# A decoder layer on one core: turning h for the down products by VectorE and a trip through DRAM instead of by TensorE

## The reference

```python
def swiglu(h, w_gate, w_up, w_down):
    return (jax.nn.silu(h @ w_gate) * (h @ w_up)) @ w_down
x = x + 0.5 * swiglu(rmsnorm(x, norm_ffn1[i]), w1_gate[i], w1_up[i], w1_down[i])
```

## Time and profile before

| what | value |
|---|---|
| median of 3 runs | 2013.55 us (2013.05 to 2016.1) |
| the profiled execution's own time | 2014.49 us |
| its span in the profile | 2012.7 us |
| granted TensorE clock, mean | 0.997 |
| PE busy | 1979.8 us (98%) |
| DVE busy | 1506.6 us (75%) |
| ACT busy | 1071.8 us (53%) |
| POOL busy | 233.3 us (12%) |

### The profile page before, as it was taken

One profiled execution on the slowest core, in us unless ns is written; L12 is line 12 of the kernel. 1 busy time (PEld: TensorE's weight loads), 2 busy tenths in 40 slices (PEclk: granted clock), 3 DMA queues, 4 the chain that ended last, 5 costly groups with the idle time before them and its releaser, 6 DMA issues.

```text
span 2012.7 us, 28994 instructions
## 1 busy us (share of the span) xinstructions
PE 1979.8 (98%) x11176; PEld 1638.6 (81%) x11176; DVE 1506.6 (75%) x1324; ACT 1071.8 (53%) x1043; POOL 233.3 (12%) x190
## 2 busy tenths in 40 slices
PE   8999999999999999999898999999999999999999
PEld 6788888888888889888787888888888888888887
DVE  5987787778878755766788546988878777787664
ACT  4655555555555556855344346555555555555553
POOL 0000000000000000344432000000000000000000
PEclk9999999999999999999998999999999999999999
DMA  7587668776787756667312555678766877677854
GB/s 249 195 242 232 215 220 249 230 232 211 235 239 233 216 174 219 198 191 222 120 42 71 173 188 168 197 241 241 237 213 209 250 234 234 211 234 231 239 178 147
DMA packets 214636, 415.69 MB, mean 207 GB/s; under 512 B 11207, under 2 KB 21059, under 8 KB 214557
## 3 DMA queue, kind: packets, MB, share of 16 engines
q1 hardware_dynamic: 189116, 361.48, 52.9%
q0 software_dynamic: 25440, 53.09, 13.9%
HBM read 363.94 MB, written 5.52 MB: 184 GB/s over the span
## 4 chain that ended last, share of the span: by engine, by line
PE 90%; DVE 7%; issue 2%; ACT 1%; DMA 0%; SPq 0%; DVEq 0%; ACTq 0%
PE PS L466 14%; PE PS L468 14%; PE PS L467 14%; PE PS L541 8%; PE PS L543 8%; PE PS L542 8%; PE PS L559 6%; PE PS L558 6%; PE PS L560 6%; PE PS L1638 2%; DVE wlo L426 2%; PE PS L521 1%; PE PS L487 1%; ACT t_hi L448 1%; DVE t_lo L453 0%
## 5 line engine op out<-in xcount | busy, mean ns | idle before, releaser
L426 DVE TENSOR_TENSOR wlo<-raw,whi 128x2048 fp32r<-128x2048 f32 (+2 forms) x338 | 732.5, 2167 | 337.3 <-PE PS L468 271.3
L417 ACT ACTIVATE whi<-raw 128x2048 fp32r<-128x2048 f32 (+2 forms) x338 | 606.0, 1794 | 217.2 <-PE PS L468 137.2
L541 PE MATMUL PS<-whi,xT_hi 128*128 128x512 f32 x768 | 303.8, 396 | 4.9 <-issue 3.2
L543 PE MATMUL PS<-whi,xT_lo 128*128 128x512 f32 x768 | 300.8, 392 | 0.0
L542 PE MATMUL PS<-wlo,xT_hi 128*128 128x512 f32 x768 | 299.4, 390 | 0.0
L466 PE MATMUL PS<-whi,hT_hi 128*128 128x512 f32 x680 | 267.6, 394 | 0.6 <-DVE wlo L426 0.4
L448 ACT ACTIVATE t_hi<-T 128x2048 fp32r<-128x2048 f32 x80 | 153.7, 1922 | 214.2 <-DVE T L443 214.2
L468 PE MATMUL PS<-whi,hT_lo 128*128 128x512 f32 x680 | 265.2, 390 | 0.0
L467 PE MATMUL PS<-wlo,hT_hi 128*128 128x512 f32 x680 | 264.8, 389 | 0.0
L1391 POOL DMA_DIRECT2D x_resid<-xs x80 | 96.1, 1202 | 1196.5 <-ACT xs L694 1159.9
L453 DVE TENSOR_TENSOR t_lo<-T,t_hi 128x2048 fp32r<-128x2048 f32 x80 | 183.4, 2292 | 31.6 <-ACT t_hi L448 31.6
(11 more groups left out here) (383 smaller groups left out, 2786.3 us busy)
## 6 DMA issues: line engine op xcount, KB each, us to landing
raw<-in_w_up SPq DMA_DIRECT2D x176, 512.0 KB, 4.0
raw<-in_w_gate SPq DMA_DIRECT2D x176, 512.0 KB, 4.9
raw<-in_w_down SPq DMA_DIRECT2D x88, 1024.0 KB, 5.1
x_resid<-xs POOLq DMA_DIRECT2D x80, 512.0 KB, 6.9
raw<-in_w_in SPq DMA_DIRECT2D x28, 1024.0 KB, 5.5
raw<-in_w_out SPq DMA_DIRECT2D x16, 1024.0 KB, 5.1
raw<-in_w_ple_gate SPq DMA_DIRECT2D x16, 1024.0 KB, 5.2
raw<-in_w_q_b SPq DMA_DIRECT2D x3, 1024.0 KB, 5.7
```

What stands on the lines that cost most here:

```text
L417: nc.scalar.activation(whi[:, n % WHI, a:wd], raw[:, n % RAW, a:wd], ACT.Copy).then_inc(hi_ready, 1)
L426: nc.vector.tensor_tensor(wlo[:, n % WLO, a:wd], raw[:, n % RAW, a:wd], f32(whi[:, n % WHI, a:wd]), ALU.subtract).then_inc(lo_ready, 1)
L541: nc.tensor.matmul(PS[:, bank, :], a, whi[:, n % WHI, c], start=first, stop=False)
L543: return nc.tensor.matmul(PS[:, bank, :], b, whi[:, n % WHI, c], start=False, stop=last)
```

## The change

PE no longer transposes groups 0 to 9 of each FFN. DVE transposes h in 32 x 32 blocks with two instructions (`h_turn` on DVE) into a new tile `h_quads`; POOL issues one transfer of it to DRAM (`store_h`, 512 KB) and, once that has landed, four transfers back (`load_hT`, 128 KB each, one for each quarter of the partitions) into `hT`, which lies over the first half of G. From there ACT makes `hT_hi` at step 4 of the pass and DVE `hT_lo` at step 5, instead of at step 0. PE waits for `hT_ready` ahead of the first down block. The last group is still transposed by PE (`last_h_turn`).

```diff
-        def h_turn(pe, f, i, it=0, b=2):
...
@@ pe_units
-                    if (i, v) == (0, 0):
-                        h_turn(pe, f, 0)
+                if (i, v) == (0, 1):
+                    pe.wait_ge(h_ready, NFF * f + 1)
...
-                if v == 1:
-                    pe.wait_ge(hT_ready, NFF * f + i + 1 + it)
@@ down
+                if j == 0:
+                    pe.wait_ge(hT_ready, NFF * f + i + 1 + it)
@@ pe_pass
             if i:
-                pe.wait_ge(x_evac, evacs(f, i - 1, 1) + 4 * it)
-                h_turn(pe, f, i, it)
@@ ACT
+        def hT_part_hi(act, f, i, it=0):
+            act.wait_ge(hT_moved, 64 * trips(f, i) + 64 * it)
+            if i:
+                act.wait_ge(block_used, FFN_BASE[f] + PAIRS + 12 * i + 12 * it)
+            nc.scalar.activation(by_quads(hT_hi[:, :, :].rearrange("p k s -> p (k s)")),
+                                 hT[:, :, :, :].rearrange("p a n c -> p n a c"), ACT.Copy).then_inc(hT_hi_ready, 1)
+        def store_h(engine, f, i, it=0):
+            engine.wait_ge(h_turned, trips(f, i) + it)
+            engine.dma_start(h_dram, h_quads[:, :, :, :, :].rearrange("p q k t r -> p (q k t r)")).then_inc(h_stored, 16)
+        def load_hT(engine, f, i, it=0):
+            engine.wait_ge(h_stored, 16 * trips(f, i) + 16 * it)
+            for q in range(4):
+                engine.dma_start(hT[32 * q:32 * q + 32, :, :, :].rearrange("p a n c -> p a (n c)"),
+                                 h_dram[:, q * 256:(q + 1) * 256].rearrange("(a r) x -> r a x", a=4)).then_inc(hT_moved, 16)
@@ act_pass
+                if s == 4:
+                    hT_part_hi(act, f, i, it)
@@ DVE
+        def h_turn(dve, f, i, it=0):
+            dve.wait_ge(h_ready, NFF * f + i + 1 + it)
+            for t in range(TT):
+                ins = nc.vector.transpose(h_quads[:, :, :, t, :].rearrange("p q k r -> p k q r"),
+                                          h[:, t, :].rearrange("p (k q r) -> p k q r", k=FKT, q=4))
+            ins.then_inc(h_turned, 1)
@@ dve_pass
-                if s == 0 and i:
-                    hT_part_lo(dve, f, i, it)
+                if s == 5:
+                    hT_part_lo(dve, f, i, it)
...
                 if s == 8:
                     hidden(dve, f, i, it)
+                    if not turn_next:
+                        h_turn(dve, f, i + 1, it)
@@ dve_ffn
             first_hidden(dve, f, B)
+            h_turn(dve, f, 0)
@@ pool_add_x
+            store_h(pool, f, 0)
+            load_hT(pool, f, 0)
             for i in range(NFF - 1):
                 for j in range(4):
+                    if i < NFF - 2 and j in (1, 2):
+                        (store_h, load_hT)[j - 1](pool, f, i + 1)
                     pool.wait_ge(x_evac, evacs(f, i, j))
```

More of the change, by code:

```diff
@@ L208, in phase @@
             base[0] = R0
+        G0 = base[0]
         G = sb("G", [P, 4, COLS])
+        hT = sb("hT", [P, 4, FKT * TT, 32], at=G0)
         TLO0 = base[0]
@@ L230, in hybrid_layer @@
         tok = sb("tok", [P, TT, TOKEN_FORMS, P], at=XS0)
+        h_quads = sb("h_quads", [P, 4, FKT, TT, 32])
         phase()
@@ L593, in pe_units, with last_h_turn @@
                 seven_product(m, P5, True, first, last).then_inc(block_used, 1)
+        def last_h_turn(pe, f):
+            pe.wait_ge(h_ready, NFF * f + NFF)
+            for j in range(FKT):
+                for t in range(TT):
+                    ins = nc.tensor.transpose(PS[:, j // 2, (j % 2) * SEQ + t * P:(j % 2) * SEQ + (t + 1) * P],
+                                              h[:, t, j * P:(j + 1) * P], ident)
+            ins.then_inc(last_h_turned, 1)
         def down(pe, f, i, it=0, last=False, turn_next=False):
@@ L676, in silu, with trips, by_quads, last_hT_part_hi @@
             ins.then_inc(silu_ready, 1)
-        def hT_part_hi(act, f, i, it=0, dst=None, b=2):
-            act.wait_ge(h_turned, NFF * f + i + 1 + it)
-            nc.scalar.activation((dst or hT_hi)[:, :, :].rearrange("p (b j) s -> p b (j s)", b=2), PS[:, b:b + 2, :],
-                                 ACT.Copy).then_inc(hT_hi_ready, 1)
+        def trips(f, i):
+            return (NFF - 1) * f + i + 1
+        def by_quads(a):
+            return a.rearrange("p (n a c) -> p n a c", n=FKT * TT, a=4)
+        def hT_part_hi(act, f, i, it=0):
[4 more added lines that the diff above has]
+                                 hT[:, :, :, :].rearrange("p a n c -> p n a c"), ACT.Copy).then_inc(hT_hi_ready, 1)
+        def last_hT_part_hi(act, f):
+            act.wait_ge(last_h_turned, f + 1)
+            nc.scalar.activation(last_hT_hi[:, :, :].rearrange("p (b j) s -> p b (j s)", b=2), PS[:, 0:2, :],
+                                 ACT.Copy).then_inc(hT_hi_ready, 1)
+        def store_h(engine, f, i, it=0):
[6 more added lines that the diff above has]
+                                 h_dram[:, q * 256:(q + 1) * 256].rearrange("(a r) x -> r a x", a=4)).then_inc(hT_moved, 16)
         def first_sum(act, f, i, it):
@@ L727, in act_pass @@
                 split_hi(act, n + s + 2, it)
-                if s == 0 and not i:
-                    hT_part_hi(act, f, 0)
+                if s == 4:
+                    hT_part_hi(act, f, i, it)
                 if s == 3 and not i:
@@ L793, in hidden, with hT_part_lo, last_hT_part_lo @@
             ins.then_inc(h_ready, 1)
-        def hT_part_lo(dve, f, i, it=0, dst=None, hi=None, b=2):
-            dve.wait_ge(hT_hi_ready, NFF * f + i + 1 + it)
-            nc.vector.tensor_tensor((dst or hT_lo)[:, :, :].rearrange("p (b j) s -> p b (j s)", b=2), PS[:, b:b + 2, :],
-                                    f32((hi or hT_hi)[:, :, :]).rearrange("p (b j) s -> p b (j s)", b=2),
-                                    ALU.subtract).then_inc(hT_ready, 1)
+        def h_turn(dve, f, i, it=0):
+            dve.wait_ge(h_ready, NFF * f + i + 1 + it)
+            for t in range(TT):
+                ins = nc.vector.transpose(h_quads[:, :, :, t, :].rearrange("p q k r -> p k q r"),
+                                          h[:, t, :].rearrange("p (k q r) -> p k q r", k=FKT, q=4))
+            ins.then_inc(h_turned, 1)
+        def hT_part_lo(dve, f, i, it=0):
+            dve.wait_ge(hT_hi_ready, NFF * f + i + 1 + it)
+            flat = "p k s -> p (k s)"
+            nc.vector.tensor_tensor(by_quads(hT_lo[:, :, :].rearrange(flat)), hT[:, :, :, :].rearrange("p a n c -> p n a c"),
+                                    by_quads(f32(hT_hi[:, :, :]).rearrange(flat)), ALU.subtract).then_inc(hT_ready, 1)
+        def last_hT_part_lo(dve, f):
+            dve.wait_ge(hT_hi_ready, NFF * f + NFF)
+            banks = "p (b j) s -> p b (j s)"
+            nc.vector.tensor_tensor(last_hT_lo[:, :, :].rearrange(banks, b=2), PS[:, 0:2, :],
+                                    f32(last_hT_hi[:, :, :]).rearrange(banks, b=2), ALU.subtract).then_inc(hT_ready, 1)
         def update_x(dve, n, j, factor, it=0):
```

13 lines of the change are left out of this document (5 added, 8 removed).

## The result

The changed kernel takes 2035.92 us (median of 5 runs, 2032.69 to 2036.79), against 2013.88 us for the kernel before beside it: ratio 1.0105, 95% interval 1.0092 to 1.0119. It is **slower by 1.05%**; the forecast was 0.68% faster.

What follows compares the result with a forecast made beforehand. PE was taken to bound the kernel, with DVE slower in the first passes: 2014.49 - 15.7 + 1.3 + 0.8 = 2000.9 us, or 2000.0 us as a median 0.9 us lower; range 1996 to 2008 us (chance 0.8).

Steps and rivals of the forecast that it cites:

- What bounds the kernel, and what PE gives back: PE bounds the kernel; dropping its transposes saves 0.87 us in each of 18 later passes, 15.7 us in all.
- DVE in the steady pass, ACT, hT: Steady passes: DVE's added transposes (1.42 us), its moved remainder and ACT's copy cost nothing; hT lands well before ACT asks.
- The first pass: First pass of each FFN: DVE sets PE's time, so the added transposes cost +1.3 us, in FFN 2 +0.8 us.
- 3.1 us fits: Down blocks: a pass's added 1.05 MB takes 3.1 us of transfer time (5.5 upper end), within a weight block's room.
- a cover of 4 us: Weight blocks: estimated room before lateness reaches PE, 4 us; 1.5 us until ACT moves.
- rival 3: Weights come late from the added megabyte in the full stretch: 1.5 us in each of 18 passes, 2027 us; chance 0.08.
- The trip's own transfer time: Store and loads of one pass: 3.1 to 5.5 us of all engines, lower end taken.
- The average share of a pass, 0.82: Transfer engines' mean share of a steady pass, expected to rise from 0.76 to 0.82 (0.86 at the upper end).
- the forecast's sum: Whole kernel: 2000.9 us for an execution like the profiled one, 2000.0 us for the median, -0.68%.

Runs made afterwards that it cites:

- Without the trip: The changed kernel with the store and four loads left out, ACT and DVE reading h_quads itself (wrongly placed values): 1998.0 us, ratio 0.9912.
- the trip added to before: The kernel before, PE's transposes kept, plus the same store and four loads on POOL's queue for a spare tile nothing reads: 2031.3 us, ratio 1.0088.
- the trip late: The changed kernel with store and loads issued by POOL behind all four additions of the pass instead of between them: 1997.2 us, ratio 0.9910.
- Experiments 9 and 10: 9: the changed kernel, loads moved behind the third addition, ahead of the fourth, 2026.8 us; 10: the changed kernel without the store for groups 1 to 9, 2011.9 us.

## Why the prediction was wrong

**What bounds the kernel, and what PE gives back: right.** Without the trip, steady passes fall from 64.06 to 63.13 us, 0.93 for the 0.87 forecast.

**DVE in the steady pass, ACT, hT: right.** The transposes cost 1.31 us for 1.42, PE does not wait at down block 2 or 3, and the later remainder of hT costs nothing.

**The first pass: right.** PE there, from the trace of the changed kernel, at `t_lo` of block 1 and at down block 1:

```profile
70.16 0.50 PE L555 MATMUL PS<-t_hi,more_hi 128*128 128x512 f32 x1 [1.15 <-DVE t_lo L458]
...
110.95 0.47 PE L471 MATMUL PS<-whi,hT_hi 128*128 128x512 f32 x1 [0.24 <-DVE wlo L431]
```

It resumes at 70.16, as in the earlier trace rows, and reaches down block 1 at 110.95 instead of 109.73: +1.2 us for +1.3. In FFN 2 the same stretch, from h to the first combining sum, grew from 37.64 to 38.38 us, +0.7 for +0.8.

**The step that failed: "3.1 us fits", under Transfers.** It put the lateness of a weight block equal to the added transfer time, 3.1 us (5.5 at the upper end), against a cover of 4 us. The cover was set too low (the runs give about 5.2), but the lateness was set far lower: 7.5 us. The room was worked out for one load, with the 5.1 us that a down block's load takes; the second half of block 3 took 7.6 us in the kernel before already. So rival 3 happened, and at more than its price. It was priced at 1.5 us in each of 18 passes on top of the forecast; against the run without a trip a pass grew by 2.26 us in FFN 1 (65.39 against 63.13) and by 2.38 in FFN 2. It was given 0.08.

The trip's own transfer time was right: q0 was busy for 16.8% of 2035.0 us instead of 13.9% of 2012.7, which is 3.1 us for each of 20 trips. Why 3.1 us of work made 7.5 us of delay can be read from POOL's queue and from both queues' shares. POOL issued the store, the four loads and the third addition:

```profile
244.69 0.58 POOL L702 DMA_DIRECT2D h_scratch<-h_quads  x1 [0.17 <-issue]
...
251.46 2.26 POOL L708 DMA_DIRECT2D hT<-h_scratch  x4 [1.37 <-DMA h_scratch<-h_quads]
...
254.43 1.23 POOL L1437 DMA_DIRECT2D x_resid<-xs  x1 [0.71 <-ACT xs L722]
```

The loads stand directly ahead of the third addition. What the queues moved (packets, MB, share) from 7.5 us after the first combining sum until block 3's weights had landed: the kernel before (237.96 to 259.58), then the changed kernel (241.96 to 271.04), then q0 in the same stretch with the trip added to before (240.33 to 268.83):

```profile
q1 hardware_dynamic: 2366, 4.58, 57.7%
...
q0 software_dynamic: 817, 1.58, 42.1%
```

```profile
q0 software_dynamic: 1424, 3.15, 52.0%
...
q1 hardware_dynamic: 2482, 4.80, 50.1%
```

```profile
q0 software_dynamic: 1424, 3.15, 53.6%
```

An addition is 0.52 MB. Before, three additions were served ahead of block 3's weights; now it is the trip and all four. By the shares, q0's packets took 15.1 us of all engines instead of 9.1, 6.0 us more: 3.1 for the trip and 2.9 for the fourth addition, as much as q0 took for that addition in the kernel before (33.3% of the 8.7 us from 256.4 to 265.1). The weights' packets took 14.6 instead of 12.5 us, and 0.22 MB of that belongs to the next block. Before, the fourth addition had hardly begun, since q0 moved next to nothing from 256.4 to 259.6, when the weights landed (a share over 100% reads as full):

```profile
q1 hardware_dynamic: 618, 1.20, 101.6%
...
q0 software_dynamic: 16, 0.01, 2.5%
```

How the two queues share the engines shows in the 10 us from 259 to 269 in the changed kernel, up to 2 us before the landing, and in the last 7.5 us before it in the kernel before:

```profile
q0 software_dynamic: 622, 1.29, 66.4%
...
q1 hardware_dynamic: 670, 1.30, 42.2%
```

```profile
q1 hardware_dynamic: 951, 1.85, 66.9%
...
q0 software_dynamic: 274, 0.53, 40.8%
```

In the changed kernel each queue got nearly as many packets as the other, 622 and 670, the additions' packets cost more, and the weights moved at 1.30 MB in 10 us, 0.13 MB/us; before, q0 had stretches with next to nothing to do and the weights moved at 1.85 MB in 7.5 us, 0.25 MB/us. The Trainium skill, "DMA: Bandwidth & Descriptors", section "SWDGE vs HWDGE vs iDMA", says that each transfer engine serves its internal queues in turn. The trace agrees, with these 622 and 670 packets. The shares by stretch (columns as in the earlier trace rows):

```profile
241.90:258.20 16.30, 16.30 (x73) 13.47 (x73) 11.73 (x10) 8.18 (x6) 6.43 (x8) 1.00 0.97 270
...
258.20:274.00 15.80, 15.80 (x71) 12.72 (x69) 9.23 (x7) 6.40 (x5) 1.20 (x1) 1.00 1.07 300
...
274.00:290.00 16.00, 14.55 (x63) 11.39 (x62) 15.14 (x10) 10.98 (x7) 0.00 (x0) 1.00 0.64 216
```

The engines were full for the down blocks before as well; now they are full for the next 16 us too. That by itself costs nothing: with the trip late the same stretch reads

```profile
254.60:270.40 15.80, 15.80 (x71) 12.97 (x71) 12.91 (x8) 9.85 (x6) 4.00 (x6) 1.00 1.04 317
```

and PE does not wait in it. What differs is what is served ahead of block 3's load. Before, the load had landed when the fourth addition was just beginning (29.1 against 34.6 us for that addition's landing, after the first sum). Now the store, the loads and the additions behind them push it back, it shares the engines with all of the fourth addition, and it lands after that (36.6 against 36.0). The trip's 3.1 us were in my text; the fourth addition's 2.9 us were not. That the fourth addition makes up this part is worked out from these bytes and landings. Experiments 9 and 10 go with it (with the loads alone q0 moved 2.62 MB before block 3's weights landed, the loads and all four additions); no run took that addition away. The rest of the 7.5 us, some 1.5, lies in the weights' own packets and is not taken apart. It is not the later start of block 1's load: with the trip added to before there is none, q0 moved the same 3.15 MB, and the weights were 7.4 us late all the same (36.2 against 28.8).

The average share of a pass, 0.82, was used to say that it would fit. It came out at 0.81 and meant nothing: what stood ahead of one load decided.

**The account** of the profiled executions: first passes +1.2 and +0.7, nine periods of FFN 1 +11.9 and of FFN 2 +13.1, the stretch between the FFNs -4.7, in all +22.3 us (2014.49 to 2036.79). The last term is not explained: in the other kernels that stretch was 1.8 to 4.8 us shorter than in the profiled execution of before too, also in the one that only added the trip, so it may be that one execution. No run was made for it. It also accounts for most of the difference between the late trip's 1997.2 us and the forecast's sum.

## What to carry to other kernels

A transfer that feeds nobody for 25 us can still be on the path, by what it stands ahead of: issue such a trip behind the traffic that recurs (here the additions), not as early as its data allows. Do not judge spare transfer capacity by the mean of a loop, nor by how full a stretch is: list what is served ahead of the load that the bottleneck waits for. Here that came to the trip and one more addition of another queue, and the load's delay (7.5 us) was over twice the trip's own transfer time (3.1). And first measure by how much a load may be late (here an estimated 5.2 us): below that everything was free, above it each microsecond was paid nearly in full.

## What the runs showed of the hardware that was not expected

- In a stretch where both queues had work throughout, packets of weights (q1) and of accumulating additions (q0) were served nearly one for one, 670 and 622 in 10 us, and the weights ran at 0.13 MB/us; with q0 next to idle (16 packets against 618) they moved 1.20 MB in 3.2 us, 0.38 MB/us.
- Two 512-column fp32 block transposes on DVE took 1.31 us, and the four 128 KB loads cost POOL 0.57 us each to issue, 2.26 us for all four.
- A trip of 1 MB, and a second MB of stores behind it, were free in a loop whose transfer engines are busy for three quarters of the time (0.76), once they stood behind the additions.
